# Seven places of a hand-ordered two-block kernel: the order in which DVE, ACT and POOL work beside TensorE

## The chip, the cores and the metric

One core of a Trainium2 chip runs the whole program. The metric is the device time of one execution in microseconds (us). Engines: PE is TensorE, PEld its weight load, DVE is VectorE, ACT is ScalarE, POOL is GpSimd, SP is the engine that issues the transfers of weights.

## The reference, cut to what matters

Two transformer blocks follow one another on 512 tokens (the first on 528, with 16 meta tokens ahead) of width 1024.

```python
# first block, two layers: one wide projection feeds three attentions
proj = rmsnorm(x, norm_g) @ w_in                  # a_q, a_k, a_v, a_f, a_z, b_..., c_..., gates
log_cum = cumsum(log_sigmoid(a_f + b_f))          # "forget": bias b_f is added, then exp, ln, cumulative sum
y_a = causal_attention(a_q, a_k, a_v, log_cum)
y_b = causal_attention([qB_nope, rope(qB_rope)], [kvB_nope, rope(b_kr)], v_b)   # qB = rms(b_cq) @ w_uq
y_c = sliding_window_attention(rope(c_q), rope(c_k), c_v, sinks)
x = x + sum(sigmoid(gates) * (branches @ w_branch)) @ w_out
# second block, i = 0, 1
y = mixer_ab(h) if i == 0 else mixer_c(h)
h = h + rms(y); h = h + rms(relu(rms(h) @ w_mlp_in) ** 2 @ w_mlp_out)
h = h + sigmoid(h @ w_ple_gate) * (p[i] @ w_ple_proj)         # "ple"
# mixer_c: an index picks at most 128 keys for each query
q   = rms(cq) @ w_uq          # 16 heads of 64 + 32, of which 32 are rotated
qi  = partial_rope(rms(cq) @ w_qi)                            # 8 index heads, 32 of 64 columns rotated
score = sum_h w_h * relu(qi_h @ ki.T)                         # then top_k(score, 128)
o   = softmax(q_full @ [ckv, k_rope].T over the picked keys) @ ckv @ w_uv
```

## The kernel before, in words

One function, `schedule()`, states the whole work as a list of `do(...)` items; each engine replays the list and runs the items that are its own, in list order. So the order in which items are written is the order on every engine, and an item that waits holds up all that stand behind it on its engine.

Nearly all of TensorE's work is matrix products with weights. Weights are fetched by SP in panels of up to 512 columns (`raw`, four slots). Each panel is split in two parts of reduced precision: the high part `wh` by ACT (L1552), and then the low part `wl` = raw - wh by DVE (L1739) or, while `splitter[0]` is "pool", by POOL (L2160). `begin_panel(j)` splits panel j+2. `wh` and `wl` have four slots, so the split of panel j waits until PE has read panel j-4. The activations are kept in two parts too (`Hh`, `Hl`, or `Yh`, `Yl`). One step of a product is three matmuls: Hh*wh (L2201), Hl*wh (L2202), Hh*wl (L2203); for products with tokens on the output partitions the three stand in L2197 to L2199. They write PSUM banks (`pp`), which DVE or ACT read out (the "evacuation") before the bank is used again.

Seven stretches matter here, named A to G below.

- **A and B**, the first projection of layer 0 and of layer 1 in the first block. A panel holds the 8 forget columns and the rotated key columns. For each of the two 264-token tiles DVE runs `forget in` (L1897 multiply, L1899 add the bias, into `Z`) and `rope32` (L1828 to L1836, through `tmp` into `M`). Then DVE evacuates query heads (L1784, `Q`). POOL fills two rows of `K` once (`ones rows`, L2137), ACT computes the exponential of `forget exp` (L1635).
- **C**, the query and key tiles of mixer_ab: DVE's `rotary` items, with two halves on POOL (L2165, L2167), and POOL also splits the low parts.
- **D**, the first gated product, ple(0): for each of eight tiles ACT runs a tanh (L1656) on PSUM, DVE L1950 and L1952 update `X`, and from it `mult_parts` makes the next product's operands: ACT Yh (L1601) and a copy of the squares' input (L1564), DVE L1751 and Yl (L1761).
- **E**, index queries of mixer_c. `rope_heads` rotates four heads at once on DVE (`rope four`, L1845 to L1854, through `tmp`), and POOL copies the four results to their places (`heads out`, L2152, four copies in one item). The next `rope four` waits for these copies, since they read the same `tmp`. `key ropes` (L2144) copies the rotated key to eight heads. Then the index products start, whose operands `M` POOL has written.
- **F**, the latent queries of the first group of heads (`latent`), beside the index scores: `rounds(i)` picks keys for query tile i: 16 times the eight largest (L2102) and their replacement (L2104), all on DVE.
- **G**, the second group: `second_group` starts with `key_ropes(1)`, ahead of `latent(1)`.

## Time and profile before

| what | value |
| --- | --- |
| times of three runs | 2815.93, 2816.07, 2829.91 us |
| median | 2816.07 us |
| time of the profiled execution | 2832.1 us |
| its span, first to last instruction | 2830.3 us |
| PE busy | 2705.7 us, 96% of the span |
| DVE, ACT, POOL busy | 1551.3, 1146.2, 144.0 us |

The profiled execution is 16.0 us above the median of the three runs and 2.2 us above the slowest of them; 1.8 us of its time lie outside its span. The share of PE says how little time is left in which PE stands still: 2830.3 less 2705.7 is 124.6 us in all, and the stretches A to G hold a part of it. Busy time of PE is counted also where the granted clock was half, so that a stretch with PE always busy may still be a slow one: the windows of the trace show the clock of each stretch.

### The profile page before, as it was taken

How to read it: one execution, taken by the hardware profiler on the slowest of the kernel's cores; microseconds unless marked ns; L12 is line 12 of the kernel's file. 1: busy time of each engine (PE TensorE's matmuls, PEld its weight loads, DVE VectorE, ACT ScalarE, POOL GpSimd, SP SyncE). 2: the span in 40 equal slices, each digit the busy share in tenths (PEclk: the TensorE clock that was granted, in tenths of full speed). 3: DMA queues.
4: the chain of work that ended last, by engine and by line, in shares of the span. 5: the costliest groups of instructions: out<-in, count | busy, mean ns of one | idle time of the engine just before them, and what ended most of it. 6: DMA issues, size and time to landing. Idle time of an engine off the chain costs nothing. (4 is left out here: it accounts for less than half of the span.)

```text
span 2830.3 us, 40756 instructions
## 1 busy us (share of the span) xinstructions
PE 2705.7 (96%) x15752; PEld 2228.2 (79%) x15752; DVE 1551.3 (55%) x3320; ACT 1146.2 (40%) x2530; POOL 144.0 (5%) x154
## 2 busy tenths in 40 slices
PE   7999999999999999999998999999999889999998
PEld 7879879899888777768786677888775657788887
DVE  5365556555545555555577463443566774633346
ACT  4345332533333532343435553332444554532233
POOL 1001000000100100000014000000003400000000
PEclk9999999999999999999999999999998989999999
DMA  3201212122220211223221122333321102233232
GB/s 128 83 26 53 64 38 83 55 74 88 81 80 24 73 57 57 79 64 89 89 79 50 45 86 86 97 97 96 91 76 40 49 1 71 79 97 97 97 93 93
DMA packets 115265, 205.33 MB, mean 73 GB/s; under 512 B 13824, under 2 KB 23680, under 8 KB 114944
## 3 DMA queue, kind: packets, MB, share of 16 engines
q1 hardware_dynamic: 113920, 198.60, 23.0%
q10 hardware_dynamic: 1152, 4.14, 0.4%
q8 instruction: 124, 2.03, 0.3%
q14 instruction: 69, 0.57, 0.1%
HBM read 200.51 MB, written 2.10 MB: 72 GB/s over the span
## 5 line engine op out<-in xcount | busy, mean ns | idle before, releaser
L2201 PE MATMUL pp<-Hh,wh 128*128 128x512 f32 (+1 forms) x2336 | 870.1, 372 | 54.9 <-DVE Hl L1761 18.0
L2203 PE MATMUL pp<-Hh,wl 128*128 128x512 f32 (+1 forms) x2336 | 808.6, 346 | 0.0
L2202 PE MATMUL pp<-Hl,wh 128*128 128x512 f32 (+1 forms) x2336 | 808.1, 346 | 0.0
L1739 DVE TENSOR_TENSOR wl<-raw,wh 128x512 fp32r<-128x512 f32 (+2 forms) x724 | 470.9, 675 | 404.3 <-ACT wh L1552 392.7
L1552 ACT ACTIVATE wh<-raw 128x512 fp32r<-128x512 f32 (+2 forms) x774 | 450.9, 605 | 348.0 <-PE pp L2203 290.6
L2201 PEld LDWEIGHTS pp<-Hh,wh 128*128 128x128 f32 x2336 | 449.0, 192 | 151.1 <-issue 33.4
L2202 PEld LDWEIGHTS pp<-Hl,wh 128*128 128x128 f32 x2336 | 450.3, 193 | 54.6 <-issue 6.2
L2203 PEld LDWEIGHTS pp<-Hh,wl 128*128 128x128 f32 x2336 | 448.2, 192 | 52.3
L2201 PE MATMUL pp<-Yh,wh 128*128 128x512 f32 (+1 forms) x1222 | 456.0, 373 | 3.0 <-DVE wl L1739 1.8
L2202 PE MATMUL pp<-Yl,wh 128*128 128x512 f32 (+1 forms) x1222 | 436.4, 357 | 0.0
L2203 PE MATMUL pp<-Yh,wl 128*128 128x512 f32 (+1 forms) x1222 | 436.4, 357 | 0.0
L2201 PEld LDWEIGHTS pp<-Yh,wh 128*128 128x128 f32 x1222 | 230.2, 188 | 49.9 <-issue 10.9
L2203 PEld LDWEIGHTS pp<-Yh,wl 128*128 128x128 f32 x1222 | 229.9, 188 | 33.8
L2202 PEld LDWEIGHTS pp<-Yl,wh 128*128 128x128 f32 x1222 | 230.4, 189 | 32.7 <-issue 2.2
L1661 ACT ACTIVATE P<-P,st 128x256 f32<-128x256 f32 (+7 forms) x280 | 148.9, 532 | 138.9 <-DVE st L1970 138.6
L2249 PE MATMUL pp<-K,Q 64*128 64x256 f32 (+16 forms) x624 | 182.2, 448 | 2.2 <-DVE st L1970 2.2
L1672 ACT ACTIVATE PT<-pp 128x256 f32<-128x256 f32 (+3 forms) x188 | 75.8, 403 | 251.7 <-PE pp L2261 250.9
L2261 PE MATMUL pp<-con,P 128*128 128x128 f32 x616 | 116.8, 279 | 9.4 <-ACT PT L1672 8.5
L1646 ACT ACTIVATE Yh<-tmp 128x512 fp32r<-128x512 f32 x64 | 40.5, 632 | 186.1 <-DVE tmp L1925 186.1
L1936 DVE TENSOR_TENSOR M<-pp,M 128x512 f32<-128x512 f32 x56 | 38.7, 692 | 139.1 <-PE pp L2203 138.0
L2160 POOL TENSOR_TENSOR wl<-raw,wh 128x512 fp32r<-128x512 f32 (+2 forms) x50 | 57.4, 1148 | 1107.9 <-PE pp L2221 567.3
L2261 PEld LDWEIGHTS pp<-con,P 128*128 128x128 f32 x616 | 77.3, 143 | 38.7 <-ACT PT L1672 23.7
(260 smaller groups left out, 2842.9 us busy)
## 6 DMA issues: line engine op xcount, KB each, us to landing
raw<-in_w SPq DMA_DIRECT2D x698, 256.0 KB, 2.7
raw<-in_w SPq DMA_DIRECT2D x36, 192.0 KB, 2.4
raw<-in_w SPq DMA_DIRECT2D x40, 128.0 KB, 2.0
out<-X SPq DMA_DIRECT2D x8, 256.0 KB, 2.0
con<-in_con ACTq DMA_DIRECT2D x1, 1513.0 KB, 11.2
X<-in_x SPq DMA_DIRECT2D x2, 528.0 KB, 5.9
X<-in_x ACTq DMA_DIRECT2D x2, 528.0 KB, 6.8
Z<-in_p ACTq DMA_DIRECT2D x2, 512.0 KB, 3.4
```

What stands on the lines that cost most here:

```text
L1552: e.activation(part("wh", j), landing(j), AF.Copy).then_inc(*act.up("split", j))
L1646: e.activation(it.hi, it.q, AF.Square).then_inc(*act.up())
L1661: e.activation(p.p, p.p, AF.Exp, bias=p.neg, scale=-1.0, accum_out=p.sum).then_inc(*act.up("exp", it.u))
L1672: e.activation(it.pt[:, 0:w], it.b4[:, 0:w], AF.Copy).then_inc(*act.up("turned", it.u))
L1739: e.tensor_tensor(part("wl", j), landing(j), part("wh", j).bitcast(F), ALU.subtract).then_inc(*dve.up("split", j))
L1936: e.tensor_tensor(it.y, it.ps, it.y, ALU.add).then_inc(*dve.up("evac", it.n))
L2160: e.tensor_tensor(part("wl", j), landing(j), part("wh", j).bitcast(F), ALU.subtract).then_inc(*pool.up("split", j))
L2201: e.matmul(it.ps, wh, xh, start=it.first, stop=False)
L2202: e.matmul(it.ps, wh, xl, start=False, stop=False)
L2203: e.matmul(it.ps, wl, xh, start=False, stop=it.end).then_inc(*pe.up())
L2249: e.matmul(p.sc, p.q, p.k[:, p.cut:it.ext], start=True, stop=True).then_inc(*pe.up("scores", it.u, x))
L2261: e.transpose(it.b4[:, 128 * x:128 * x + 128], it.p[:, o:o + 128], it.ident).then_inc(*pe.up("turn", it.u))
```

## The change

The list of items for PE and for SP keeps its order; DVE, ACT and POOL get theirs changed in seven places.

- A, B: the bias is added in one item over 528 columns, `forget bias`, later; in layer 1 a third pair of query heads comes in `lead`, so that panel splits stand between the evacuations.
- C: from the last key tile of `rotary` on, DVE splits the low parts, where POOL did.
- D: a tile's Yh, Yl and squares are issued behind the tanh and the X update of the next tile (`carry_on`).
- E: `heads out` becomes four items of one copy, one issued at each `begin_panel`; what is left is issued before the next `rope four`. Index queries and the latent queries of both groups in mixer_c use this. Seven steps of `keys(0)` stand ahead of the mark for which the index products wait, where four did.
- E, G: `key ropes` becomes eight items of one copy; for the first group they stand in the latent steps, for the second one at every other step.
- F: no pick is made in the first 18 steps, and one at each step after.

```diff
--- before.py
+++ after.py
@@ -135,6 +135,7 @@
         split_to(j + WS - 2)
+        head_home()
@@ -552,24 +553,30 @@
+    def head_home():
+
+        if four.get("wait"):
+            four["out"] = do("heads out", **four["wait"].pop(0))["n"]
+            tmp_turned["at"] = ("pool", "heads out", four["out"])
+
     def heads_home():
-
-        if four.get("wait"):
-            four["out"] = do("heads out", **four.pop("wait"))["n"]
-            tmp_turned["at"] = ("pool", "heads out", four["out"])
-
-    def rope_heads(name, l, starts, x, ranges, ready, dsts, before, by_pool=False):
+        while four.get("wait"):
+            head_home()
+
+    def rope_heads(name, l, starts, x, ranges, ready, dsts, before, by_pool=False, in_pieces=False):
         p, q = tmp[:, 0, :], tmp[:, 1, :]
...
                 split_to(done["split"])
+            heads_home()
             given, four["out"] = four["out"], None
...
             if by_pool:
-                four["wait"] = dict(q=q[:, a:b], dsts=[d[:, a:b] for d in dsts], n_in=n, before=before)
-                heads_home()
+                four["wait"] = [dict(q=q[32 * x:32 * x + 32, a:b], dst=d[:, a:b], n_in=n, before=before) for x, d in enumerate(dsts)]
+                if not in_pieces:
+                    heads_home()
             return ("dve", "four read", n)
@@ -577,12 +584,10 @@
             for n in (0, 2):
-                for k, _ in enumerate(gemm_steps(panel(name, l, K3, [c for h in hs[n:n + 2] for c in cols(96 * h, 64)]), x, 3, ranges, ready,
-                                                 two_heads(Q, i + n, None, before))):
-                    if n == 2:
-                        heads_home()
-                    yield
-            yield from rope_heads(name, l, [96 * h + 64 for h in hs], x, ranges, ready, [Q[64:96, i + n, :] for n in range(4)], before, by_pool)
+                yield from gemm_steps(panel(name, l, K3, [c for h in hs[n:n + 2] for c in cols(96 * h, 64)]), x, 3, ranges, ready,
+                                      two_heads(Q, i + n, None, before))
+            yield from rope_heads(name, l, [96 * h + 64 for h in hs], x, ranges, ready, [Q[64:96, i + n, :] for n in range(4)], before, by_pool,
+                                  headed is None)
             if headed is not None:
@@ -707,7 +712,7 @@
         def fgate(ps, a, b, t):
-            do("forget in", cum=cum[:, a:b], ps=ps[0:8], rs=rs[0:8, a:b], bias=sm[0:8, B_F + l:B_F + l + 1], t=t, before=before)
+            do("forget in", cum=cum[:, a:b], ps=ps[0:8], rs=rs[0:8, a:b], t=t, before=before)
             return rope32(ps, 64, kr[:, a:b], a, b, t, rs, before)
@@ -716,11 +721,17 @@
         heads = [(list(cols(128 * c, 128)), QR, two_heads(Q, 2 * c, rs, before)) for c in range(some)]
-        lead(chunk_major("w_in", l, gates + heads, Hx, 8, hr), lambda: qk(Q, 0, some, QR), produce, N, rs)
+        behind_heads = [(Q, 0, c, QR) for c in range(some, 2 * some)]
+
+        def next_heads():
+            for args in behind_heads:
+                yield from qk(*args)
+        lead(chunk_major("w_in", l, gates + heads, Hx, 8, hr), next_heads, produce, N, rs)
         filled = do("ones rows", q=Q[64:66, :, :], k=K[64:66, :, :], before=before, gates=mark())["n"]
+        rest = [(Q, 0, c, QR) for c in range(2 * some, 4)] + [(K, 512, c, TOKR) for c in range(4)]
+        run(qk(*rest.pop(0)))
+        do("forget bias", cum=cum, bias=sm[0:8, B_F + l:B_F + l + 1])
         forget = mark()
-        rest = [(Q, 0, c, QR) for c in range(some + 1, 4)] + [(K, 512, c, TOKR) for c in range(4)]
-        run(qk(*rest.pop(0)))
         do("forget exp", cum=cum, w1=w1, forget=forget)
@@ -1041,14 +1052,23 @@
         given = [None] * 2
-        tiles = []
+        tiles, waiting = [], []
+
+        def carry_on():
+            for c, n in waiting:
+                ready[c] = mult_parts(N, X2[:, c, :], MIX_PRE + 8 + c, Yx[c], ("dve", "ple", n), before)
+                caught_up()
+            waiting.clear()
+
         for c in range(8):
...
                 if i == 0:
-                    ready[c] = mult_parts(N, X2[:, c, :], MIX_PRE + 8 + c, Yx[c], ("dve", "ple", n), before)
-                    caught_up()
+                    carry_on()
+                    waiting.append((c, n))
+                    if c == 7:
+                        carry_on()
                 else:
@@ -1169,6 +1189,8 @@
                 for c in range(4):
+                    if dst is K and c == 3:
+                        splitter[0] = "dve"
                     for n, _ in enumerate(rotary(dst, 4, c, c0, later)):
@@ -1275,11 +1297,9 @@
             hs = range(i, i + 4)
-            for k, _ in enumerate(gemm_steps(panel("w_qi_2", 0, K3, [c for h in hs for c in cols(64 * h + 32, 32)]), cqx, 3, ALLR, ready["q"], plain(i))):
-                if k == 1:
-                    heads_home()
-                yield
-            yield from rope_heads("w_qi_2", 0, [64 * h for h in hs], cqx, ALLR, ready["q"], [M[64 * (h % 2):64 * (h % 2) + 32, h, :] for h in hs], before, True)
+            yield from gemm_steps(panel("w_qi_2", 0, K3, [c for h in hs for c in cols(64 * h + 32, 32)]), cqx, 3, ALLR, ready["q"], plain(i))
+            yield from rope_heads("w_qi_2", 0, [64 * h for h in hs], cqx, ALLR, ready["q"], [M[64 * (h % 2):64 * (h % 2) + 32, h, :] for h in hs], before, True,
+                                  True)
         splitter[0] = "pool"
@@ -1316,8 +1336,8 @@
-        def key_ropes(g, before):
-            do("key ropes", ks=[k[64:96, :] for k in Ks[g]], kr=kr, before=before)
+        def key_rope(g, h, before):
+            do("key ropes", ks=[Ks[g][h][64:96, :]], kr=kr, before=before)
         before0 = mark()
@@ -1327,7 +1347,7 @@
         ahead_of = keys(0, summed)
-        for _ in range(4):
+        for _ in range(7):
             next(ahead_of)
@@ -1355,7 +1375,6 @@
             next(products)
-        key_ropes(0, before0)
@@ -1371,14 +1390,18 @@
                 run(made)
+                heads_home()
                 there = mark()
...
             next(made)
+            if n < 8:
+                key_rope(0, n, before0)
             for _ in range(1 + n % 3 % 2):
                 next(products, None)
-            if n > 1 and n % 2:
+            if n >= 18:
                 next(first, None)
+        next(first)
         run(made)
@@ -1399,8 +1422,10 @@
             here = mark()
-            key_ropes(1, here)
-            yield from latent(1, M, here)
+            for n, _ in enumerate(latent(1, M, here)):
+                if n % 2 and n < 16:
+                    key_rope(1, n // 2, here)
+                yield
             yield from keys(1, here)
@@ -1895,6 +1920,8 @@
         e.tensor_tensor(it.cum, it.ps, it.rs, ALU.mult).then_inc(*dve.up())
+
+    def forget_bias(it):
         dve.wait_ge("dve")
@@ -2148,8 +2175,7 @@
             pool.wait_ge(other, "mark", it.before)
-        for x, dst in enumerate(it.dsts):
-            e.tensor_copy(dst, it.q[32 * x:32 * x + 32, :]).then_inc(*pool.up("heads out", it.n))
+        e.tensor_copy(it.dst, it.q).then_inc(*pool.up("heads out", it.n))
```

Line numbers in the changed kernel are higher by 25 to 27 in the engines' functions (L1739 becomes L1764, L1784 L1809, L1899 L1926, L2152 L2178, L2160 L2186, L2144 L2171, L1656 L1681, L1601 L1626, L1564 L1589).

**B, on DVE**, in layer 1, before from the second forget tile on. `Z` is the forget row, `Q` and `K` the heads, `wl` a low part. Before:

```order
L1897 TENSOR_TENSOR Z<-pp,rs 8x264
L1899 TENSOR_SCALAR Z<-Z,sm 8x264 [waits dve]
L1828 TENSOR_TENSOR tmp<-pp,con 32x264 [waits dve]
L1829 TENSOR_TENSOR tmp<-pp,con 32x264
L1834 TENSOR_TENSOR tmp<-tmp 32x264 [waits dve]
L1836 TENSOR_TENSOR M<-tmp,rs 32x264 [waits dve]
L1784 TENSOR_TENSOR Q<-pp,rs 64x512 [waits pe]
L1784 TENSOR_TENSOR Q<-pp,rs 64x512 x5
L1739 TENSOR_TENSOR wl<-raw,wh 128x512 [waits act] x2
L1784 TENSOR_TENSOR Q<-pp,rs 64x512 [waits pe]
L1784 TENSOR_TENSOR Q<-pp,rs 64x512
L1739 TENSOR_TENSOR wl<-raw,wh 128x512 [waits act] x2
```

And of the change, where the second forget tile ends with its copy to `M` right ahead of the first row:

```order
L1809 TENSOR_TENSOR Q<-pp,rs 64x512 [waits pe]
L1809 TENSOR_TENSOR Q<-pp,rs 64x512
L1764 TENSOR_TENSOR wl<-raw,wh 128x512 [waits act]
L1809 TENSOR_TENSOR Q<-pp,rs 64x512 x2
L1764 TENSOR_TENSOR wl<-raw,wh 128x512 [waits act]
L1809 TENSOR_TENSOR Q<-pp,rs 64x512 x2
L1809 TENSOR_TENSOR Q<-pp,rs 64x512 [waits pe]
L1809 TENSOR_TENSOR Q<-pp,rs 64x512
L1764 TENSOR_TENSOR wl<-raw,wh 128x512 [waits act] x2
L1809 TENSOR_TENSOR K<-pp,rs 64x264 [waits pe]
L1809 TENSOR_TENSOR K<-pp,rs 64x264
L1809 TENSOR_TENSOR K<-pp,rs 64x264 [waits pe]
```

The bias (L1899 before) has left both forget tiles and stands two rows below the second piece. Of the two splits that stood behind six evacuations of `Q` one stands now behind two, the other behind four.

**D, on ACT**, the first tiles of ple(0). `tmp<-pp` is the tanh, `Yh` and `K` belong to `mult_parts`, `wh` is a high part. Before:

```order
L1656 ACTIVATE tmp<-pp 128x512 [waits pe]
L1601 ACTIVATE Yh<-X,sm 128x512 [waits dve]
L1564 ACTIVATE K<-X 128x512
L1552 ACTIVATE wh<-raw 128x512 [waits pe,w1]
L1656 ACTIVATE tmp<-pp 128x512
L1601 ACTIVATE Yh<-X,sm 128x512 [waits dve]
L1564 ACTIVATE K<-X 128x512
L1656 ACTIVATE tmp<-pp 128x512 [waits pe]
L1601 ACTIVATE Yh<-X,sm 128x512 [waits dve]
L1564 ACTIVATE K<-X 128x512
L1552 ACTIVATE wh<-raw 128x512 [waits w2]
```

And of the change:

```order
L1681 ACTIVATE tmp<-pp 128x512 [waits pe] x2
L1626 ACTIVATE Yh<-X,sm 128x512 [waits dve]
L1589 ACTIVATE K<-X 128x512
L1577 ACTIVATE wh<-raw 128x512 [waits pe,w1]
L1681 ACTIVATE tmp<-pp 128x512
L1626 ACTIVATE Yh<-X,sm 128x512 [waits dve]
L1589 ACTIVATE K<-X 128x512
L1681 ACTIVATE tmp<-pp 128x512 [waits dve,pe]
L1626 ACTIVATE Yh<-X,sm 128x512
L1589 ACTIVATE K<-X 128x512
```

The tanh of a tile now stands ahead of the Yh of the tile before it, and each `wh` behind the Yh and K of one tile less.

**E, on POOL**, around the second four copies of the index heads (`M`) and the first key ropes (`K<-V`). Before:

```order
L2160 TENSOR_TENSOR wl<-raw,wh 128x256 [waits pe,act,pool]
L2152 COPY M<-tmp 32x512 [waits dve,pool]
L2152 COPY M<-tmp 32x512 x3
L2160 TENSOR_TENSOR wl<-raw,wh 128x256 [waits pe,act,pool] x2
L2152 COPY M<-tmp 32x512 [waits dve,pool]
L2152 COPY M<-tmp 32x512 x3
L2160 TENSOR_TENSOR wl<-raw,wh 128x256 [waits pe,act,pool]
L2160 TENSOR_TENSOR wl<-raw,wh 128x384 [waits pe,act,pool] x2
L2144 COPY K<-V 32x512 [waits pool] x8
```

And of the change, from behind the first copy of the first four:

```order
L2186 TENSOR_TENSOR wl<-raw,wh 128x256 [waits pe,act,pool]
L2178 COPY M<-tmp 32x512 [waits pool]
L2186 TENSOR_TENSOR wl<-raw,wh 128x256 [waits pe,act,pool]
L2178 COPY M<-tmp 32x512 [waits pool] x2
L2178 COPY M<-tmp 32x512 [waits dve,pool]
L2186 TENSOR_TENSOR wl<-raw,wh 128x256 [waits pe,act,pool]
L2178 COPY M<-tmp 32x512 [waits pool]
L2186 TENSOR_TENSOR wl<-raw,wh 128x384 [waits pe,act,pool]
L2178 COPY M<-tmp 32x512 [waits pool]
L2186 TENSOR_TENSOR wl<-raw,wh 128x384 [waits pe,act,pool]
L2178 COPY M<-tmp 32x512 [waits pool]
L2186 TENSOR_TENSOR wl<-raw,wh 128x384 [waits pe,act,pool]
```

Each four copies in a row have become single copies with splits between them: the first four have two splits among them, the second four three.

## Rows read from the trace of the kernel before

**Rows 1.** page: the span, and busy us (share of the span) x instructions.

```profile
span 2830.3 us, 40756 instructions
...
PE 2705.7 (96%) x15752; PEld 2228.2 (79%) x15752; DVE 1551.3 (55%) x3320; ACT 1146.2 (40%) x2530; POOL 144.0 (5%) x154
```

**Rows 2.** PE's waits, 28 to 62 us (A): us in total, times, longest.

```profile
PE pp L2201 <- DVE tmp L1829: 3.4, 1, 3.4
```

**Rows 3.** DVE, 38 to 49 us (A): start us, us, line, operation, shapes.

```profile
38.80 0.35 DVE L1899 TENSOR_SCALAR Z<-Z,sm 8x264 f32<-8x264 f32 x1
...
41.49 2.78 DVE L1899 TENSOR_SCALAR Z<-Z,sm 8x264 f32<-8x264 f32 x1
...
44.78 0.43 DVE L1829 TENSOR_TENSOR tmp<-pp,con 32x264 f32<-32x264 f32 x1
```

**Rows 4.** POOL in time, 36 to 60 us (A), the same columns.

```profile
40.51 3.61 POOL L2137 MEMSET K<- 2x4224 f32 x1 [28.55 <-PE pp L2203]
```

**Rows 5.** windows (A): stretch, its us, busy us, PEclk, DMA share, GB/s.

```profile
44.00:52.00 8.00, 6.74 (x42) 6.74 (x43) 7.52 (x17) 2.13 (x3) 0.13 (x1) 0.79 0.06 7
```

**Rows 6.** PE's waits, 735 to 785 us (B).

```profile
PE pp L2201 <- DVE wl L1739: 5.2, 1, 5.2
```

**Rows 7.** DVE in time, 745 to 764 us (B).

```profile
748.02 2.25 DVE L1899 TENSOR_SCALAR Z<-Z,sm 8x264 f32<-8x264 f32 x1
...
752.15 4.28 DVE L1784 TENSOR_TENSOR Q<-pp,rs 64x512 f32<-64x512 f32 x6
756.46 1.29 DVE L1739 TENSOR_TENSOR wl<-raw,wh 128x512 fp32r<-128x512 f32 x2
```

**Rows 8.** windows, 756 to 764 us (B).

```profile
756.00:764.00 8.00, 6.79 (x36) 6.80 (x37) 4.39 (x7) 6.26 (x8) 0.00 (x0) 0.60 0.42 131
```

**Rows 9.** POOL in time, 1535 to 1575 us (C).

```profile
1545.44 1.28 POOL L2167 TENSOR_TENSOR K<-K,tmp 128x512 f32<-128x512 f32 x1
1546.80 1.59 POOL L2160 TENSOR_TENSOR wl<-raw,wh 128x512 fp32r<-128x512 f32 x1
```

**Rows 10.** PE's waits, 1535 to 1575 us (C).

```profile
PE pp L2197 <- POOL wl L2160: 2.5, 2, 2.2
```

**Rows 11.** PE's waits, 2062 to 2100 us (D).

```profile
PE pp L2201 <- DVE wl L1739: 4.1, 2, 3.3
```

**Rows 12.** ACT in time, 2068 to 2082 us (D); idle before in brackets.

```profile
2075.24 0.72 ACT L1601 ACTIVATE Yh<-X,sm 128x512 fp32r<-128x512 f32 x1 [1.48 <-DVE X L1952]
```

**Rows 13.** windows, 2078 to 2086 us (D).

```profile
2078.00:2086.00 8.00, 8.00 (x25) 6.35 (x26) 6.98 (x11) 4.53 (x8) 0.00 (x0) 0.66 0.24 66
```

**Rows 14.** POOL in time, 2140 to 2162 us (E).

```profile
2148.60 0.78 POOL L2160 TENSOR_TENSOR wl<-raw,wh 128x256 fp32r<-128x256 f32 x1 [1.38 <-issue]
2150.05 2.62 POOL L2152 COPY M<-tmp 32x512 f32<-32x512 f32 x4 [0.68 <-DVE st L2082]
2152.75 2.89 POOL L2160 TENSOR_TENSOR wl<-raw,wh 128x256 fp32r<-128x256 f32 x3
```

**Rows 15.** PE in time, 2153 to 2156 us (E).

```profile
2155.10 0.79 PE L2330 MATMUL pp<-V,M 64*128 64x256 f32 x1
```

**Rows 16.** windows, 2155 to 2175 us (E).

```profile
2155.00:2175.00 20.00, 20.00 (x46) 9.87 (x45) 10.76 (x18) 7.08 (x17) 8.01 (x11) 0.50 0.17 54
```

**Rows 17.** PE's waits, 2175 to 2225 us (F, G).

```profile
PE pp L2197 <- DVE tmp L1846: 4.9, 1, 4.9
PE pp L2201 <- POOL wl L2160: 2.5, 1, 2.5
```

**Rows 18.** DVE groups by form, 2170 to 2206 us (F): busy us, mean ns.

```profile
L2102 DVE MAX8 st<-Z 128x8 f32<-128x256 f32 x12 | 5.1, 428 | 0.4
L2104 DVE MATCH_REPLACE8 Z<-st,Z 128x256 f32<-128x256 f32 x12 | 4.9, 408 | 0.0
```

**Rows 19.** windows, 2200 to 2208 us (F).

```profile
2200.00:2208.00 8.00, 7.88 (x23) 6.23 (x24) 5.11 (x15) 1.80 (x3) 3.43 (x5) 0.61 0.09 26
```

**Rows 20.** POOL in time, 2162 to 2220 us (G).

```profile
2209.25 5.29 POOL L2144 COPY plain<-V 32x512 f32<-32x512 f32 x8 [3.92 <-DVE st L1970]
```

More of the change, by code:

```diff
@@ L2117, in vector_program @@
             "two_heads": two_heads, "rope64": rope64, "ropes": ropes, "rope halves": rope_halves, "rope32": rope32, "rope four": rope_four, "zgate": zgate, "gate": gate,
-            "proj": proj, "add_quarter": add_quarter, "forget in": forget_in, "forget sum": forget_sum, "forget rows": forget_rows,
+            "proj": proj, "add_quarter": add_quarter, "forget in": forget_in, "forget bias": forget_bias, "forget sum": forget_sum, "forget rows": forget_rows,
             "rows there": rows_there, "relu2": relu2, "relu2 low": relu2_low, "add_out": add_out, "add_normed": add_normed, "final": final, "ple": ple, "scores": scores,
```

## The prediction

> **What bounds the kernel now.** I read the page first. PE is busy for 2705.7 of 2830.3 us [rows 1]: TensorE is the bound, and it stands still for 124.6 us in all. So no order on the other engines can bring more than these 124.6 us and what the clock loses, and each of the seven places is worth what PE waits there. The second view is PE's own list of waits, stretch by stretch; the third is the timeline of the engine that it waited for, which tells what kept that engine; the fourth are windows behind each long wait, because busy time hides slow matmuls. The reader should see in the waits one long entry for each place: 3.4 us in A [rows 2], 5.2 in B [rows 6], 2.5 in C [rows 10], 4.1 in two waits in D, the longest 3.3 [rows 11], 4.9 in F and 2.5 in G [rows 17]. The windows show that the granted clock falls behind a stall: 0.79 on the mean in the 8 us behind A [rows 5], 0.60 behind B [rows 8], 0.66 behind D [rows 13], 0.61 behind F [rows 19]. Of the two levels, 1.2 and 2.4 GHz, these are mixtures. I price that as busy time times (1 - clock): 6.74 x 0.21 = 1.4 us in A, 6.79 x 0.40 = 2.7 in B, 8.00 x 0.34 = 2.7 in D, 7.88 x 0.39 = 3.1 in F.
>
> **A, the bias of layer 0.** The same instruction took 0.35 us at 38.80 and 2.78 at 41.49 [rows 3], and the second lies under POOL's MEMSET, 40.51 to 44.12 [rows 4]: it ended at 44.27, when the MEMSET did. The bank that PE waited for is given free by L1829 at 44.78. The change takes both bias items out ahead of it, so that L1829 starts some 2.8 + 0.4 us earlier, about 41.6, and ends at 42.0; PE goes on when it ends, 44.78 + 0.43 = 45.2, and so began to wait at 45.2 - 3.4 = 41.8. That leaves a stall of about 0.2. The bias returns as one item later, and ACT's exponential with the splits behind it too; two splits come late for PE, by an estimate of 1.1 and 0.9 us (the order of the change replayed with the trace's durations; these are the weakest terms). Sum: 3.4 + 1.4 - 0.2 - 2.0 = 2.6 gained, between 1.2 (clock not given back) and 4.6 (splits in time).
>
> The Trainium skill, "SBUF — State Buffer", section "SBUF: two separate sides", says that VectorE and GpSimd share one pair of ports as an exclusive lock for the whole instruction. The 2.78 us agree: the bias ended when the MEMSET did. By the same rule a split moved from POOL to DVE in C would be held by each of POOL's halves still there, up to 1.29 us, and C would give 1.2 and not 2.5.
>
> **B, the same in layer 1, and a split moved forward.** Here the bias took 2.25 us [rows 7], then six evacuations of Q run for 4.28 us, and only then the two low parts, at 756.46, for the first of which PE waits 5.2 us [rows 6]. In the change a low part stands behind two evacuations (1.4 us). The second tile's chain ends 2.3 + 0.4 us earlier, at about 749.5, so that this low part is done at 749.5 + 1.4 + 0.65 = 751.6, and PE, which went on at 756.46 + 0.65 = 757.1, began to wait at 757.1 - 5.2 = 751.9: nothing is left of the stall. The next item that is late is a split behind the bias, 0.6 us by the replay. Gain 5.2 + 2.7 - 0.6 = 7.3; without the clock 4.6.
>
> **C, POOL's splits.** POOL's second rope half at 1545.44 ends at 1546.72, and the split behind it takes 1.59 us [rows 9]; PE waits for it and once more, 2.5 us in all [rows 10]. DVE makes the same low part in 0.65 us (1.29 for two, [rows 7]) and, as its 55% of the span say, has room more often than not [rows 1]. Gain 2.5, with 0 as the lower bound, if DVE's own evacuations come to stand in front.
>
> **D, ple(0).** ACT's Yh waits for DVE's X update, idle for 1.48 us at 2075.24 [rows 12], while the next tanh and the next high part stand behind it; that is once per tile, eight times. The chain tanh, X, Yh, high part, low part is longer than PE's time for a tile, and the low part falls behind tile by tile until it is 3.3 us late [rows 11]. With the tanh a tile ahead, ACT no longer stands still between them; it has some 10 us (7 x 1.5) more room, three times the stall. What takes the wait's place: the Yh and Yl of tile 7 come last, at the same distance from their tanh as before, so the second, short wait (4.1 - 3.3 = 0.8) stays. Gain 3.3 + 2.7 = 6.0; 3.3 without the clock; the least is 0, if the tanh then waits for the `tmp` that DVE still reads.
>
> **E, index heads in pieces.** This one costs. Before, POOL split at 2148.60, copied the second four heads in 2.62 us at 2150.05, and split three panels in 2.89, 0.96 each [rows 14]; the index products started at 2155.10 [rows 15]. In the change two splits stand among the first four copies, the second of them that of 2148.60. So the last copy ends at about 2148.6 + 0.8 + 2 x 0.65 = 2150.7, or half a microsecond before that if the split starts as soon as its high part is there. Only then may `rope four` overwrite `tmp`. It takes some 3.1 us (between four and five DVE operations of 0.7), then come four copies and three splits, 2.6 + 2.9 = 5.5. The last copy, for which the index products wait, ends at about 2159.1 against 2155.1: a loss of 4.0. The lower bound is 0 (if the products could start on the heads that are there; their mark forbids it), the upper 4.0 plus what a longer stall takes in clock. In the 20 us behind the start the clock was 0.50 already, PE busy throughout [rows 16], which costs 10 us before as after; if the stretch grows with the longer stall I take 5 more.
>
> **F, the picks.** Twelve picks lay in the latent steps, each MAX8 0.428, a load, and MATCH_REPLACE8 0.408 [rows 18], about 0.95 us; four of them stood in a row ahead of `rope four`, for which PE waited 4.9 us [rows 17]. They go, 3.8 us. But `rope four` now needs the four pieces before it, which stand between three 512-column splits of POOL, and each of those waits for ACT; by the replay it starts 0.5 us earlier only. Gain 0.5; the bounds are 0 and, were the pieces there in time, 4.9 + 3.1 = 8.0.
>
> **G, the key ropes of the second group.** POOL copies eight in 5.29 us at 2209.25 [rows 20], and a split behind them is 2.5 us late for PE [rows 17]. One copy at a time never holds a split for more than 0.66 us. Gain 2.5. **Later**, another `rope four` waits for a piece behind a split (0.7), and the picks that were moved lie in the attention stretch, where DVE has little idle time (0.5): loss 1.2, from 0 to 4.
>
> **Sum.** 2.6 + 7.3 + 2.5 + 6.0 + 0.5 + 2.5 = 21.4 gained, 4.0 + 1.2 = 5.2 lost: 16.2. It is made against the profiled execution, 2832.1 us (span 2830.3 and 1.8 around it), so 2815.9; that execution is 16.0 above the median of 2816.07 though no place of it names the reason, so I put the same 16.2 on the median: 2799.9, say **2800**.
>
> **The rivals.**
> 1. *The forecast*, 2800, own range 2795 to 2804. Chance 0.33.
> 2. *The stalls go, the clock doesn't come back.* Shorter stalls may still let it fall, or it falls elsewhere. For it: the clock is low at 2155 to 2175 with PE always busy [rows 16], so that a stall isn't all that decides. Against it: A, B, D each show it right behind the stall. Without 1.4 + 2.7 + 2.7 the gain is 9.4: 2806.7. Chance 0.23.
> 3. *E is dearer*: the longer wait for the last piece lengthens the half-clock stretch by 5 us and the next rope comes late too (2). The gain is 16.2 - 7 = 9.2: 2806.9. Chance 0.15.
> 4. *The pieces are in time in F* and its stall goes with its clock: 7.5 more, 2792. For it: POOL is idle for long between its splits. Chance 0.15.
> 5. *Gains of A, B and D are taken back by the next wait* (ACT's high parts stand close behind everywhere), so that only C, G and half of the others stay, 12 less 5: 2809. Chance 0.09.
> 6. *Slower*: POOL's pieces. Each `rope four` waits for a piece that waits behind a split, which waits for ACT's high part, which waits for PE. It happens at three ropes in E, F and later. It decides if each costs over 16.2 / 3 = 5.4 us beyond what is counted; a stall as in F with its clock costs 8.0, three make 24, and the time is 2816 - 16 + 24 = 2824. Chance 0.05.
>
> The Trainium skill, "TensorE: Matmul & The Clock Gate", section "Part 1: The HAM clock gate", has the clock set by how busy PE has been; rival 2 is where this decides otherwise than I priced. By this rule removing a stall gives its clock back, and the trace agrees behind A, B and D but shows nothing for 2155 to 2175.
>
> **How the numbers follow.** A measurement of this kernel tells about 0.5% from no change, that is 14.1 us: faster means under 2802.0. The forecast lies just beyond that. Rival 1 gives 0.25 faster and 0.08 same, rival 4 0.15 faster, of 2 some 0.05, of 3 0.03: with a little of 5, 0.49. Rivals 2, 3 and 5 are otherwise same, 0.46 with the rest of 1, and rival 6 with 0.05 is slower. The range goes from rival 4's value less some us of its bounds, 2788, to 2814: above and below it are left rival 6 and the ends of 4 and 5.
>
> **What would show it.** Right: no wait over 1 us on L1829 near 42 and on a low part near 752 and 2074; the bias at 0.4 us; no half clock in the 8 us behind; PE waits for POOL gone at 1548 and 2213. E: the index products start 3 to 5 us later, measured from the last panel before them. F: still a wait of 4 us or more for `rope four`, between 2185 and 2200. Wrong: other waits of PE have grown at the same places (L1599's or L1552's results), the tanh of ple(0) waits for `tmp`, or the clock at 2155 to 2175 has changed by much either way.

## The result, and the profile after

| | before | changed |
| --- | --- | --- |
| runs | 8 | 8 |
| median | 2818.49 us | 2806.71 us |
| lowest to highest | 2815.93 to 2832.03 | 2803.07 to 2812.75 |
| profiled execution, span | 2832.1, 2830.3 us | 2806.04, 2804.2 us |

The ratio is 0.9946 with a 95% interval of 0.9930 to 0.9962: 0.5% faster, 15 us with an interval of about 11 to 20. The medians differ by 11.8 us, less than the ratio says; two of the eight runs of before lie at 2830 and 2832, and they weigh on the ratio and hardly on the median. The two traces differ by 26.1 us of span; the section on the experiments shows why a pair of traces can say more than the change is worth.

The page of the changed kernel, for [rows 1]:

```profile
span 2804.2 us, 40752 instructions
...
PE 2684.2 (96%) x15752; PEld 2213.5 (79%) x15752; DVE 1552.1 (55%) x3328; ACT 1145.6 (41%) x2530; POOL 130.4 (5%) x144
```

PE stands still for 2804.2 - 2684.2 = 120.0 us, against 124.6 before: 4.6 less. The other 21.5 us of the 26.1 are busy time, so matmuls that ran at a higher granted clock: the clock was half for 134.6 us in the trace of before and for 80.1 us in this one. The list of waits alone doesn't tell this, and the busy shares (96% twice) don't show it at all.

**A and B.** VectorE in time in the changed kernel, layer 0 and layer 1, for [rows 3] and [rows 7]; then the list of PE's waits from 28 to 62 us, for [rows 2]:

```profile
40.69 0.43 DVE L1854 TENSOR_TENSOR tmp<-pp,con 32x264 f32<-32x264 f32 x1
...
745.17 1.41 DVE L1809 TENSOR_TENSOR Q<-pp,rs 64x512 f32<-64x512 f32 x2
746.61 0.69 DVE L1764 TENSOR_TENSOR wl<-raw,wh 128x512 fp32r<-128x512 f32 x1
...
755.54 0.48 DVE L1926 TENSOR_SCALAR Z<-Z,sm 8x528 f32<-8x528 f32 x1
```

```profile
PE pp L2241 <- DVE K L1776: 1.6, 1, 1.6
PE pp L2227 <- DVE wl L1764: 1.4, 2, 0.7
PE pp L2227 <- DVE tmp L1854: 0.6, 1, 0.6
```

L1854 starts at 40.69 and is done at 41.12, where L1829 was done at 45.21. In layer 0 the 3.4 us wait has become one of 0.6 and two of 0.7. The first of these two is for a low part that stands behind eight evacuations of Q, and it is there in ones_later too, where the bias is not moved; the second is for a low part for which VectorE itself waits for ScalarE's high part. The 1.6 us wait for K was there before. In layer 1 the low part stands behind two evacuations of Q; the same list from 735 to 785 us is empty. The bias takes 0.48 us for 528 columns in place of 2.25 for the second 264.

**C.** VectorE and GpSimd in time in the changed kernel, for [rows 9]; PE waits for no low part from 1535 to 1575 us of before, or 1515 to 1560 here:

```profile
1531.51 0.68 DVE L1764 TENSOR_TENSOR wl<-raw,wh 128x512 fp32r<-128x512 f32 x1
...
1534.98 3.28 DVE L1764 TENSOR_TENSOR wl<-raw,wh 128x512 fp32r<-128x512 f32 x2
```

```profile
1534.47 1.54 POOL L2191 TENSOR_TENSOR tmp<-tmp,con 128x512 f32<-128x512 f32 x1
1536.09 1.62 POOL L2193 TENSOR_TENSOR K<-K,tmp 128x512 f32<-128x512 f32 x1
```

The low part at 1531.51 started before a rope half of GpSimd and took 0.68 us; the two that started behind one take 3.28, more than twice that, and the second of them ends 0.55 us after the second half (1538.26 and 1537.71). The halves take 1.54 and 1.62 in place of 1.10 and 1.28. PE did not wait for any of them.

**D.** ScalarE in time in ple(0), for [rows 12], and PE's only wait there, for [rows 11]:

```profile
2050.37 0.71 ACT L1626 ACTIVATE Yh<-X,sm 128x512 fp32r<-128x512 f32 x1
...
2052.30 0.60 ACT L1681 ACTIVATE tmp<-pp 128x512 f32<-128x512 f32 x1 [0.69 <-PE pp L2229]
```

```profile
PE pp L2227 <- DVE wl L1764: 0.7, 1, 0.7
```

Yh no longer waits for VectorE; ScalarE waits for PE, which is how it should look when PE is the bound. The wait of 3.3 us is gone and the short one stays, at 0.7.

**E.** PE's waits from 2130 to 2165 us, the first index product on PE (for [rows 15]), and the window of 20 us from 2134 (for [rows 16]):

```profile
PE pp L2227 <- POOL wl L2186: 4.2, 1, 4.2
PE pp L2356 <- POOL M L2178: 1.5, 1, 1.5
```

```profile
2136.15 0.76 PE L2356 MATMUL pp<-V,M 64*128 64x256 f32 x1 [1.55 <-POOL M L2178]
```

```profile
2134.00:2154.00 20.00, 18.45 (x58) 9.13 (x56) 11.80 (x18) 9.73 (x23) 8.62 (x11) 0.79 0.17 47
```

The longer wait, 4.2 us, is not at the index products but one panel ahead of them: its low part stands behind the copies in pieces on GpSimd. At the products PE waits 1.5 us more for the last copy.

**F and later.** VectorE around the second rope of the latent queries, and in the attention stretch:

```profile
2164.47 1.61 DVE L2125 SCALAR_TENSOR_TENSOR Z<-P,st,Z 128x512 f32<-128x512 f32 x2
2172.01 0.01 DVE L1870 LOAD_MASK_SELECT tmp<-pp  x1 [5.93 <-POOL Q L2178]
...
2276.48 0.67 DVE L1997 CUSTOM_DVE_ANT_0 P<-pp,Z,k 128x384 f32<-128x384 f32 x1
...
2277.19 0.69 DVE L2129 MAX8 st<-Z 128x8 f32<-128x512 f32 x1
2277.92 0.09 DVE L2131 MATCH_VALUE_LOAD Z<-st,Z 128x8 f32 x1
2277.99 0.68 DVE L2131 MATCH_REPLACE8 Z<-st,Z 128x512 f32<-128x512 f32 x1
2278.59 0.19 DVE L2019 RECIPROCAL st<-st 128x8 f32<-128x8 f32 x1
```

VectorE, from which four picks were taken, now stands idle for 5.93 us until the last piece of GpSimd is there, and PE's wait for the rope is 4.6 us in place of 4.9 [rows 17]. And a reciprocal for which PE waits 2.0 us comes behind a pick of 512 columns that has nothing to do with it; before, no pick stood there any more.

**G.** PE in time at the place of the 2.5 us wait for GpSimd of [rows 17]:

```profile
2187.28 0.47 PE L2227 MATMUL pp<-Hh,wh 128*128 128x512 f32 x1 [1.25 <-ACT M L1648]
```

The wait for GpSimd is gone, but the same matmul now waits 1.25 us for a copy of ScalarE, so that 1.2 us of the 2.5 are gained there.

**A ledger of the two traces.** PE runs the same 15752 matmuls in the same order in both, so the start of the n-th in one trace less that in the other tells what was gained up to it. By stretches (times of before, us; the changed kernel less before):

```
from    to      gained (-) or lost (+)
   0    37      -1.0   no edit
  37    60      -2.8   A
  60   740      -1.8   no edit
 740   780      -5.8   B
 780  1530      -1.4   no edit
1530  1575      -3.2   C
1575  2040      -0.9   no edit
2040  2100      -6.2   D
2125  2158      +4.0   E
2158  2176      -6.4   index products
2192  2212      -1.9   F
2212  2224      -2.3   G
2224  2240      +1.6   the rope after
2240  2290      -1.2   no wait removed there
2290  2320      +4.2   late picks
2320  2825      -1.2   no edit
```

Two stretches of 0.0 are left out. The stretches without an edit, -0.9 to -1.8 each, show how much a single line may owe to the clock alone. Busy time is not the same as time gained: between 1575 and 2040 us PE's busy time fell by 3.0 us and its matmuls came 0.9 earlier.

### The profile page after: what moved, and what is told of

Read it like the earlier page. It is cut to its first block and busy times, and to the rows that moved or that the text cites. A ratio compares the mean times of both kernels' runs of the same rounds, so it can differ in the third digit from the quotient of the medians.

```text
span 2804.2 us, 40752 instructions
## 1 busy us (share of the span) xinstructions
PE 2684.2 (96%) x15752; PEld 2213.5 (79%) x15752; DVE 1552.1 (55%) x3328; ACT 1145.6 (41%) x2530; POOL 130.4 (5%) x144
## 5 line engine op out<-in xcount | busy, mean ns | idle before, releaser
L1764 DVE TENSOR_TENSOR wl<-raw,wh 128x512 fp32r<-128x512 f32 (+2 forms) x734 | 480.7, 680 | 411.7 <-ACT wh L1577 406.2
L2228 PEld LDWEIGHTS pp<-Hl,wh 128*128 128x128 f32 x2336 | 444.6, 190 | 54.0 <-issue 6.2
L2275 PEld LDWEIGHTS pp<-K,Q 64*128 64x128 f32 (+2 forms) x624 | 76.7, 188 | 31.7 <-issue 21.3
```

Source lines behind the costliest of these rows:

```text
L1764: e.tensor_tensor(part("wl", j), landing(j), part("wh", j).bitcast(F), ALU.subtract).then_inc(*dve.up("split", j))
L2228: e.matmul(it.ps, wh, xl, start=False, stop=False)
L2275: e.matmul(p.sc, p.q, p.k[:, p.cut:it.ext], start=True, stop=True).then_inc(*pe.up("scores", it.u, x))
```

## The experiments

Each ran on one chip beside the kernel before; the ratio is to it, and the median in microseconds. They ran in three sessions, each on a chip of its own: before_again, abcd, efg and no_pieces; then early3, np_early3, undo_d and ones_later; then the rest. "Before" had medians of 2820.0 to 2820.1 in them. A ratio is taken over all runs and carries the spread of before, so it can say another thing than two medians; two kernels of one session are best compared by their medians. The changed kernel did not run again: its 2806.71 us stands beside 2818.49 of before, so a difference of one or two microseconds to it says nothing.

**before_again**, no edit.

> The kernel before once more, for a second trace. Its eight runs so far lie at 2816 to 2821 us and, two of them, at 2830 and 2832; the trace at hand is of the upper kind (2832.1). Theory 1 (the clock alone makes the difference): the same stalls at the same places to 0.3 us, the granted clock low in other and in fewer stretches (134.6 us at half clock in the first trace; some 105 if the time is 2818). Theory 2 (a stall of its own makes the upper runs): one wait of PE or of a transfer of over 5 us that the other trace hasn't.

Measured: median 2821.52 (10 runs, 2815.62 to 2831.74), ratio 1.0002 (0.9984 to 1.0021). The profiled execution took 2831.74, the upper kind again. Laid beside the first trace, no matmul starts more than 0.4 us apart, and the record of the granted clock shows the same stretches, 134.5 us at half clock against 134.6. So the expected comparison of an upper with a lower run didn't come about in the traces. The mean granted clock of each run speaks for theory 1: the four of these ten runs at 2827.5 us and more have 0.976 to 0.978, the six at 2822.2 and less 0.981 or 0.982, and the other runs of before divide nearly so, with only a few in between. As an estimate from these figures, 0.976 means 136 us at half clock and 0.982 about 101; half of the difference is 17 us, for 16 between the two kinds of runs. The clock is given to three places, so this is good to some 3 us either way, and a stall of its own below that isn't ruled out. What makes the clock differ stays open. The traces do show that an execution of 2832 us can be repeated to 0.02%.

**abcd**: A to D as changed, E to G as before (the diff of the change without its parts from `index_query` on and without the pieces).

> Places A to D of the change alone (forget bias, layer 1's heads, DVE's splits in the last key tile, ple(0)'s parts one tile later); E, F and G as before. By the terms of the prediction 2.6 + 7.3 + 2.5 + 6.0 = 18.4 us less than before: 2818.5 - 18.4 = 2800, so faster than the whole change (2806.7). Rival (the second half of the change pays too, and what the first half gains is partly taken back): 2808 to 2812.

Measured: median 2803.46 (6 runs), ratio 0.9931 (0.9909 to 0.9953). Theory 1: 16.5 us by the medians, 19 by the ratio, for 18.4 expected. The first half of the change alone is at least as good as the whole, as far as these runs tell: 3.3 us better by the medians, with intervals that overlap.

**efg**: the reverse, A to D as before.

> Places E to G alone (head copies in pieces, seven key steps, picks later, key ropes one at a time); A to D as before. By the terms of the prediction 0.5 + 2.5 - 4.0 - 1.2 = 2.2 us slower than before, 2820.7, and by the late picks as the trace of the change shows them (4 us rather than 0.5) some 3 more: 2820 to 2824. Rival (the clock at the index products, half for 20.5 us before and 10.2 in the trace of the change, is this half's doing and is kept): 2812 to 2816.

Measured: median 2826.21 (12 runs), ratio 1.0018 (1.0002 to 1.0033): 5 to 6 us slower than before, 2 above what was expected. In its trace the ledger has +4.0 at E, -6.4 at the index products, -1.9 at F, -2.3 at G, +1.7 at the next rope, -1.2 from there to 2290 and +4.2 at the late picks, as in the whole change. Without the index products that is 4.5 us lost, near what the medians say; with them this trace is 8.1 us shorter than that of before, which the medians don't bear out. The rival, that E's half brings the clock and keeps it, fell by its time, and abcd, which has none of E, ran the same products faster still (below).

**no_pieces**:

```diff
-            yield from rope_heads(... [M[64 * (h % 2):64 * (h % 2) + 32, h, :] for h in hs], before, True,
-                                  True)
+            yield from rope_heads(... [M[64 * (h % 2):64 * (h % 2) + 32, h, :] for h in hs], before, True)
...
-            yield from rope_heads(... [Q[64:96, i + n, :] for n in range(4)], before, by_pool,
-                                  headed is None)
+            yield from rope_heads(... [Q[64:96, i + n, :] for n in range(4)], before, by_pool)
...
-        for _ in range(7):
+        for _ in range(4):
             next(ahead_of)
```

> The whole change, but the four head copies stay together behind their rope for index queries and latent queries, and four key steps stand ahead of the index products as before. Theory 1 (the pieces hold the next rope back): index products 4 us earlier, the wait of 4.6 us for the rope of the latent queries nearly gone, the one at the next rope (1.8) smaller; 2806.7 - 8 = 2799 or less. Rival (four copies in a row put the low parts behind them back): PE waits 2.4 and 0.8 us for POOL's low parts again and little is gained: 2804 to 2807.

Measured: median 2800.06 (6 runs), ratio 0.9924 (0.9901 to 0.9947), 6.6 us under the whole change; 8 were expected. PE's waits from 2110 to 2220 us:

```profile
PE pp L2285 <- ACT P L1684: 2.6, 1, 2.6
PE pp L2225 <- POOL wl L2184: 1.6, 1, 1.6
...
PE pp L2221 <- DVE tmp L1869: 0.7, 1, 0.7
```

The rope's wait of 4.6 us has become 0.7; the low parts cost 1.6 in place of 4.2; a new wait of 2.6 has come for the first exponential of the attention, behind the picks in a row. Theory 1 holds: the pieces held the ropes back. This run changes two things, pieces and key steps; index_together below tells the latent queries' pieces from the rest.

**early3**, on the whole change, and **np_early3**, the same edit on no_pieces:

```diff
-            if n >= 18:
+            if n >= 18 or n in (3, 5, 7):
                 next(first, None)
```

> The whole change with the same three picks at steps 3, 5 and 7, and nothing else. Theory 1: 4 us less at the attention stretch, so 2806.7 - 4 = 2802.7; the 4.6 us wait for the rope stays, since it hangs on the pieces and not on picks. Rival (picks, not pieces, time the rope): that wait grows by what three picks take, 2.9 us, and the time is 2805 or more.

> The kernel with the head copies together (2800.1 us), and in it three of the picks moved back to steps 3, 5 and 7 of the latent queries, where VectorE stands idle for 1.4 us and more between index sums. Theory 1 (nine picks leave three too many for the attention stretch, where mask and pick of 2.1 us follow each other and a reciprocal comes 2.0 us late): the wait for it goes, the 3.9 us lost between 2290 and 2320 come back, 2800 - 4 = 2796. Rival (the picks hold up index sums or the rope again, a bank is late): the 4 us are lost at 2192 to 2212 instead, 2799 to 2801.

Measured: early3 2807.59 (6 runs), ratio 0.9954 (0.9936 to 0.9972), so nothing gained over 2806.71. np_early3 2798.46 (6 runs), ratio 0.9924 (0.9906 to 0.9943), 1.6 under no_pieces, within what these medians tell. In both traces the 2.0 us wait at the late picks is gone, and the 4.2 (3.9) us between 2290 and 2320 with it, as theory 1 has it. In early3 they are lost again in other places: +4.2 at the next rope where the change had +1.6, with PE's wait for it 2.1 us in place of 1.8 and the clock at half there for 3.4 us, then 1.1 less gained at F, 1.3 less at G and 1.4 more lost between 2240 and 2290. PE's wait for the rope before it is 4.9 us, 0.3 more and not 2.9, so the rival's mechanism fell as well, though its time, 2805 or more, came. Most of these losses are in stretches with more half clock than in the trace of the change; that the early picks caused them isn't shown.

**undo_d**: the change with ple(0) as before.

> The whole change but for ple(0), whose parts follow each tile at once as before. Theory 1: the low part 3.3 us late and half clock behind it come back, 2806.7 + 6 = 2812.7. Rival (the clock is given back by other places on the average over runs): + 3.3 only, 2810.

Measured: median 2815.96 (12 runs), ratio 0.9983 (0.9971 to 0.9994): 9.3 us slower than the change, where 6 were expected; against before of its own session it is 4.1 us faster where the change was 11.8, so 7.7 slower. The 3.3 us wait is back. In the ledger D itself is worth 5.9 (6.2 less 0.3); the rest lies at other places of its trace, most of it as clock.

**ones_later**, on the kernel before:

```diff
-        filled = do("ones rows", q=Q[64:66, :, :], k=K[64:66, :, :], before=before, gates=mark())["n"]
         forget = mark()
         rest = [(Q, 0, c, QR) for c in range(some + 1, 4)] + [(K, 512, c, TOKR) for c in range(4)]
         run(qk(*rest.pop(0)))
         do("forget exp", cum=cum, w1=w1, forget=forget)
+        filled = do("ones rows", q=Q[64:66, :, :], k=K[64:66, :, :], before=before, gates=mark())["n"]
```

> The kernel before, with one item moved: GpSimd's MEMSET of two rows of K comes behind the next pair of query heads, so that it no longer runs beside the second bias instruction of either layer; the bias stays where it was. Theory 1 (the MEMSET holds the bias, nothing else does): the bias takes 0.35 us both times in both layers; the 3.4 us wait of layer 0 falls below 1 us, the 5.2 us wait of layer 1 to 3.3 (less the 1.9 that the bias was held), with the clock 3 to 6 us less in all. Rival (the second bias is slow for another reason, such as reading what was just written): it takes 2 us or more again and nothing moves.

Measured: median 2811.49 (12 runs), ratio 0.9978 (0.9959 to 0.9998). VectorE and GpSimd in time in layer 0, and PE's waits from 28 to 62 and from 735 to 785 us:

```profile
42.16 0.34 DVE L1899 TENSOR_SCALAR Z<-Z,sm 8x264 f32<-8x264 f32 x1
```

```profile
48.19 3.62 POOL L2137 MEMSET K<- 2x4224 f32 x1 [36.32 <-PE pp L2203]
```

```profile
PE pp L2201 <- DVE tmp L1829: 1.3, 2, 1.0
PE pp L2201 <- DVE wl L1739: 0.7, 1, 0.7
...
PE pp L2201 <- DVE wl L1739: 3.3, 1, 3.3
```

The second bias takes 0.34 us when the MEMSET isn't beside it, and the 5.2 us wait of layer 1 falls to exactly the 3.3 expected. In layer 0 two waits for L1829 stay, 1.3 us together with the longest 1.0, where less than 1 was expected, and 0.7 for a low part. One item moved is worth 6 us by the ratio and 8.6 by the medians. In the ledger it has 3.0 us at A, all that the change has there (2.8), and 2.7 of the 5.8 at B; the rest of B needs the low part moved forward. The MEMSET holds up nothing where it runs now: two low parts beside it take 1.29 us, as ever.

**index_together**: the change with no_pieces' first and last edit, the latent queries in pieces.

> The whole change, but the copies of the index heads alone stay together, with four key steps ahead of the index products; the latent queries keep their copies in pieces. Theory 1 (the term E of the prediction, a loss of 4.0): the index products start 4 to 5 us earlier and the 4.6 us wait for the rope of the latent queries stays: 2806.7 - 4.4 = 2802.3. Rival (the clock behind the start takes it back): the same time as the change, 2806 to 2808, with a longer stretch of half clock at the index products.

Measured: median 2806.20 (7 runs), ratio 0.9954 (0.9938 to 0.9970). The index products do start 4 us earlier, and the time is that of the change, as the rival has it. The windows over the index products, of index_together and of no_pieces:

```profile
2132.00:2153.00 21.00, 21.00 (x49) 9.97 (x47) 8.69 (x15) 6.98 (x17) 7.18 (x9) 0.51 0.18 53
```

```profile
2133.00:2148.00 15.00, 14.74 (x55) 7.49 (x54) 10.22 (x16) 7.97 (x19) 7.41 (x9) 1.00 0.24 60
```

Laid beside each other, the matmuls from the first index product to the same later one, 47 in all, up to 2176 us of before, with the time from a matmul at 2126 (of before) to the first product ahead of it:

```
kernel           until the first product   the stretch itself   of it at half clock
before, index_together   29.0, 29.1 us          21.1, 21.1 us        20.4, 20.4 us
changed, efg             33.1, 33.0             14.7, 14.7            6.3,  6.2
undo_ab, undo_d          33.0, 31.5             17.4, 16.9            12.2, 10.2
early3                   33.0                   12.6                  0
no_pieces, abcd          27.5, 27.5             13.1, 13.3            0,    0
np_early3, ones_later    27.5, 27.5             13.1, 13.3            0,    0
np_early4                29.1                   13.1                  0
```

The first column has E's mechanism, 29.1 to 33.0 or 27.5 to 31.5 us: 4.0 us for pieces. The 1.5 us between the two pairs are not in the schedule. The second column is the clock: the same matmuls take 12.6 to 21.1 us.

In before and index_together the clock fell within 0.1 us ahead of the first product and was half for 20.5 us, with PE busy throughout; in the change and efg it fell 4.0 us ahead, just behind PE's wait of 4.2 us, and stayed half for 10.2; in early3 it was back 1.1 us ahead of the first product.

The schedule doesn't decide this: index_together and no_pieces run the same instructions in the same order on every engine until GpSimd's order parts at 2168.8 and 2159.5 us, over 10 us behind the end of the stretch, and one spent 20.4 us of it at half clock, the other none. The change and early3 are the same until VectorE's order parts at 2150.9 and 2149.3, about where the stretch ends. And ones_later, with before's E to G, went through it at full clock. So no trace here can credit or charge this stretch to an edit, and the rival is right about the time of index_together, while its reason, that the earlier start brings the half clock, isn't shown: it was half for 20.4 us before the change as well.

**undo_ab**: the change with the bias and layer 1's heads as before.

> The whole change but for the forget bias and layer 1's heads. By the prediction's terms A 2.6 and B 7.3: 2806.7 + 9.9 = 2816.6. Rival (only the waits count on the median, their clock is lost elsewhere anyway: 1.2 + 4.6): 2812.5.

Measured: median 2820.21 (12 runs), ratio 0.9996 (0.9985 to 1.0008): 13.5 us slower than the change, where 9.9 were expected; by before of its own session, against which it is 0.2 us slower, 12.0. Laid against the changed kernel, its trace has lost 3.3 us by 60 us and 6.5 more between 740 and 780, 9.8 together, the forecast's sum; but 1.3 of the 3.3 lie ahead of 37 us, where nothing is edited, so the two places themselves have 8.6. At the end it is 12.0 behind.

**np_early4**, on np_early3:

```diff
-            if n >= 18 or n in (3, 5, 7):
+            if n >= 19 or n in (3, 5, 7, 13):
                 next(first, None)
```

> The kernel with copies together and three early picks (2798.5 us), with a fourth pick ahead of the second rope of the latent queries, where VectorE stands idle for 1.56 us, and one fewer behind it. Theory 1 (the 2.6 us that PE waits for the first exponential of the attention hang on the picks in a row): that wait is 1.0 us shorter, 2797.5, within what the medians tell. Rival (the pick meets an index sum that comes later, and the rope starts late): PE waits up to 1 us for the rope, 2799.

Measured: median 2796.92 (5 runs, 2794.84 to 2798.70), ratio 0.9916 (0.9899 to 0.9933). PE's waits from 2150 to 2200 us:

```profile
PE pp L2285 <- ACT P L1684: 1.6, 1, 1.6
```

The wait of 2.6 is 1.0 us shorter, which is theory 1, and the rope is waited for 0.3 us. By the median it is 1.5 us under np_early3 of another session, which these runs can't tell from nothing; it has the lowest median of this study, 9.8 us under the change.

## Why the prediction was right or wrong

The time, 2806.7, lies in the range 2788 to 2814, but outside the forecast's own 2795 to 2804, and it is to a tenth or two the number of rivals 2 and 3. "Faster" was to be under 2802.0 us; the median is above that, the ratio of 0.9946 is just beyond 0.5%, and its interval lies on both sides, so the side isn't settled. The gain was forecast as 16.2 us; the ratio says 15.2, the medians 11.8. One part of the difference is the foot that the time stood on: the median of three runs was 2816.07, that of eight 2818.49, and of 23 some 2820. The other is E to G, which were to lose 2.2 us and lost 5 to 6 in efg, while A to D brought 16.5 to 19 for 18.4. That the sum came out as near as it did is partly luck: the late picks lost 4.2 us for 0.5, and the index products gained 6.4 us of clock in the trace, which no term had.

- **A, 2.6**: 2.8 from 37 us on, of which 1.4 are waits (3.4 less 0.6 and twice 0.7) and 1.4 clock. The mechanism is shown by ones_later.
- **B, 7.3**: 5.8 between 740 and 780, and the wait of 5.2 is gone whole; the later wait of 0.6 that I added never came. What was mis-sized is its clock, 2.7 forecast and 0.6 measured: the half clock behind the stall is gone, but the changed trace has 3.4 us of it earlier, at 742 us of before. The two together, 9.9, were worth 12.0 to 13.5 by the medians of undo_ab.
- **C, 2.5**: 3.2, the same to 0.04 in nine traces with C laid beside before, and 0.0 in efg, which lacks it.
- **D, 6.0**: 6.2 in the ledger, and 7.7 to 9.3 by the medians.
- **E, -4.0**: 4.0. The chain written out (pieces behind splits, rope behind the last piece, three more splits) was right step by step: 33.1 us in place of 29.0. Its terms add up to 2159.3 and not 2159.1, which changes nothing.
- **F, +0.5**: 1.9. PE's wait went only from 4.9 to 4.6, for the reason given; the rest is clock.
- **G, +2.5**: 2.3, but not for the reason given. The sum took the whole wait of 2.5 us as gained; the next wait at the same matmul, 1.25 us for ScalarE, leaves 1.2, and the other 1.3 in the ledger is less half clock. The number came out by luck.
- **Later, -1.2**: this term was mis-sized, 1.6 for the rope (0.7 forecast) and 4.2 for the late picks (0.5 forecast). I had looked at how busy VectorE is in the attention stretch and not at what stands behind a pick there: mask and pick of 2.1 us alternate, so three more picks of 512 columns (0.69 + 0.09 + 0.68 us each, with gaps) move what follows by over 4 us, and 4.2 were lost. With three picks moved back (np_early3) the loss there is gone.
- **The clock**: priced at what it had cost behind each stall, 6.8 in all. Between the two traces PE's busy time fell by 21.5 us. Of that 6.4 are the index products, 5.0 lie behind A, B and D (1.4, 0.7 and 2.9), 3.0 at F and G (1.7 and 1.3), and the rest comes in pieces of up to 3 us, most of it at places without an edit. Rival 2 (the clock doesn't come back) has B for it, and nothing at A and D.
- **Rival 3**'s extra loss at the index products didn't come; before had the bad case already. The rope after it did come late, by 1.6 us. **Rival 4** (pieces in time in F) fell: VectorE waited 5.93 us for the last. **Rival 5** fell at A to D. **Rival 6**, the chain of pieces, is real, but efg puts E to G at 5 to 6 us slower in all, not at the 16 from which it would have decided.

VectorE and GpSimd are seen to hold each other up twice: the bias took 2.78 us with the MEMSET beside it and 0.34 without, and in C two low parts took 3.28 us beside the rope halves where 1.4 were due. The Trainium skill, "SBUF — State Buffer", section "SBUF: two separate sides", has a port pair of the two engines locked for the whole instruction, and a VectorE instruction with two inputs in SBUF needs it only against a GpSimd one that reads SBUF. Both places agree with a lock, the second low part ending just behind the second half, and so do the low parts beside the MEMSET, which reads nothing (1.29 us for two). The bias has one input in SBUF and would need the pair by what the page calls a 2-port mode; no run here shows the mode. The 1.3 us that the lock would have taken from C by my sum it did not take, because PE did not wait for these two.

What stays open: why undoing A and B, or D, costs some 2 to 5 us more on the medians than their own stretch says (the clock elsewhere and the comparison across sessions are the likely places, not shown ones), and what makes the clock of before such that it runs at 2816 or at 2832. The stretch of index products could account for 8 of these 16 us (21.1 less 13.1), but both traces of before are of upper runs, so this is only argued.

## What to carry to other kernels

Read the engine behind the wait, not the wait: a bias of 8 rows held PE for 3.4 us because a MEMSET of another engine ran beside it, and moving the MEMSET gave 6 to 8.6 us, where the rewritten order of both places gave 12 to 13.5. When a copy is cut in pieces to let something in between, ask who waits for the last piece; here that was the next rope, and the pieces cost more than the splits gained. When a wait is taken out, ask what the same matmul waits for next. A change should be undone part by part before it is kept: half of this one was worth 16 to 19 us and the other half minus 5 to 6.

## What the runs showed of the hardware that had not been expected

- The same stretch of 47 matmuls, of 64 rows by 256 and 384 columns with some of 128 by 512 among them, took 13.1 us at 2.4 GHz (no_pieces) and 21.1 us with 20.4 of them at 1.2 GHz (index_together). PE was busy for all of the longer one, and up to its end both kernels ran the same instructions in the same order on every engine.
- Two executions of before agreed to 0.4 us at every matmul with the same record of the clock, while its runs spread from 2814 to 2833 us. Its slowest runs have a mean granted clock of 0.976 or 0.977, its fastest 0.982 to 0.984. So a difference of two traces, here 26.1 us for a change worth 12 to 15, contains what the clock happened to do; a ledger of single stretches is safe only where the clock is the same on both sides.
- A MEMSET of 3.6 us held a TENSOR_SCALAR with one operand in SBUF until it ended (2.78 us for 0.34), but no TENSOR_TENSOR beside it (1.29 us for two low parts); beside GpSimd's own TENSOR_TENSOR the low parts of VectorE took 1.64 us each in place of 0.68, and GpSimd's took 1.54 in place of 1.10.
